# Order and engines at the entry of a hybrid attention and MLP block: column 0 of the scale, the squares of x, TensorE's first work

## The reference

```python
c_act = jax.nn.silu(c)
mod = c_act @ w_ada[l] + b_ada[l]
sh_a, sc_a, gt_a, sh_m, sc_m, gt_m = [m[:, None, :] for m in jnp.split(mod, N_MOD, axis=-1)]
h = rms_norm(x, g_pre_attn[l]) * (1.0 + sc_a) + sh_a
proj = h @ w_in[l]
q_a, k_a, v_a, q_b, ckv, k_pe = [proj[..., offs[i]:offs[i + 1]] for i in range(6)]
...
o = jnp.concatenate([rms_norm(o_a, g_out_a[l]), rms_norm(o_b, g_out_b[l])], axis=-1)
o = o @ w_out[l]
x = x + gt_a * rms_norm(o, g_post_attn[l])
h = rms_norm(x, g_pre_mlp[l]) * (1.0 + sc_m) + sh_m
y = jnp.square(jax.nn.relu(h @ w_mlp_in[l])) @ w_mlp_out[l]
x = x + gt_m * rms_norm(y, g_post_mlp[l])
```

## Time and profile before

| | |
|---|---|
| median of 3 runs | 2016.6 us (2016.35 to 2017.35) |
| the profiled execution, its time | 2017.13 us |
| its span in the profile | 2015.2 us |
| PE busy in the span | 1984.6 us (98%) |
| DVE, ACT busy | 1730.3 us, 1005.1 us |
| granted TensorE clock, mean | 0.998 |

### The profile page before, as it was taken

How to read it: one execution, slowest core, us unless ns; L and a number is a source line. 1 busy time by engine, 2 the same in 40 slices (tenths; PEclk the granted TensorE clock), 3 DMA queues, 4 the chain that set the end, 5 groups by cost and what they waited for, 6 DMA issues and landing times.

```text
span 2015.2 us, 30682 instructions
## 1 busy us (share of the span) xinstructions
PE 1984.6 (98%) x11171; PEld 1738.4 (86%) x11171; DVE 1730.3 (86%) x1993; ACT 1005.1 (50%) x1424; POOL 161.3 (8%) x173
## 2 busy tenths in 40 slices
PE   7999999999999999999999999999999999999998
PEld 5887888788888878999999999998888888888886
DVE  7897998788877788999999999988898898898866
ACT  6464223688733374565656565655343343434322
POOL 0000000257400000000000000000300000000000
PEclk9999999999999999999999999999999999999999
DMA  9988768600378746667676766668746546556452
GB/s 357 369 297 293 237 215 233 214 1 21 130 248 261 239 163 188 206 216 230 214 229 213 229 213 229 214 222 331 255 176 250 193 181 250 186 187 252 175 179 84
DMA packets 260180, 432.28 MB, mean 215 GB/s; under 512 B 27648, under 2 KB 155264, under 8 KB 247168
## 3 DMA queue, kind: packets, MB, share of 16 engines
q1 hardware_dynamic: 242576, 361.42, 53.1%
q0 software_dynamic: 15936, 63.97, 8.6%
q10 hardware_dynamic: 1584, 5.77, 0.8%
HBM read 367.15 MB, written 63.96 MB: 214 GB/s over the span
## 4 chain that ended last, share of the span: by engine, by line
PE 91%; DVE 5%; ACT 3%; issue 1%; DMA 0%; POOL 0%; SPq 0%; POOLq 0%; ACTq 0%; DVEq 0%
PE bank L2817 9%; PE bank L2819 9%; PE bank L2818 9%; PE bank L2839 9%; PE bank L2841 9%; PE bank L2840 9%; PE bank L2324 6%; PE bank L2326 6%; PE bank L2325 6%; PE bank L2900 1%; PE bank L2899 1%; PE bank L2898 1%; PE bank L2337 1%; PE bank L2338 1%; PE bank L2339 1%
## 5 line engine op out<-in xcount | busy, mean ns | idle before, releaser
L1367 ACT ACTIVATE hi<-w 128x1024 fp32r<-128x1024 f32 x168 | 178.4, 1062 | 264.8 <-PE bank L2841 197.8
L2839 PE MATMUL bank<-hi,y_use 128*128 128x512 f32 x784 | 306.6, 391 | 0.0
L2840 PE MATMUL bank<-lo,y_use 128*128 128x512 f32 x784 | 305.1, 389 | 0.0
L2841 PE MATMUL bank<-hi,y_use 128*128 128x512 f32 x784 | 305.1, 389 | 0.0
L1286 ACT ACTIVATE hi<-a 128x1024 fp32r<-128x1024 f32 x196 | 206.6, 1054 | 154.5 <-DVE a L2031 141.9
L2028 DVE TENSOR_TENSOR lo<-a,hi 128x1024 fp32r<-128x1024 f32 x196 | 239.1, 1220 | 43.6 <-ACT hi L1286 43.2
L2817 PE MATMUL bank<-h_hi,hi 128*128 128x256 f32 x896 | 253.7, 283 | 0.9 <-DVE c_b L2058 0.9
L2818 PE MATMUL bank<-h_lo,hi 128*128 128x256 f32 x896 | 253.6, 283 | 0.0
L2819 PE MATMUL bank<-h_hi,lo 128*128 128x256 f32 x896 | 253.6, 283 | 0.0
L819 ACT ACTIVATE hi<-raw 128x1024 fp32r<-128x1024 f32 (+2 forms) x120 | 120.5, 1007 | 230.9 <-DMA raw<-in_w_in 66.6
L2143 DVE TENSOR_TENSOR lo<-w,hi 128x1024 fp32r<-128x1024 f32 x168 | 203.9, 1220 | 32.0 <-ACT hi L1367 30.7
(11 more groups left out here) (402 smaller groups left out, 4700.5 us busy)
## 6 DMA issues: line engine op xcount, KB each, us to landing
w<-in_w_mlp_out SPq DMA_DIRECT2D x128, 512.0 KB, 4.8
a<-in_w_mlp_in SPq DMA_DIRECT2D x112, 512.0 KB, 4.5
y_use<-y_dram SPq DMA_DIRECT2D x53, 1024.0 KB, 9.3
raw<-in_w_ada SPq DMA_DIRECT2D x100, 512.0 KB, 4.7
y_dram<-y_out POOLq DMA_DIRECT2D x28, 1792.0 KB, 6.8
w_turned<-in_w_ada_t SPq DMA_DIRECT2D x32, 1024.0 KB, 7.1
raw<-in_w_out SPq DMA_DIRECT2D x32, 512.0 KB, 4.6
raw<-in_w_heads SPq DMA_DIRECT2D x32, 448.0 KB, 6.5
```

The costliest lines, as they stand in the source:

```text
L1367: nc.scalar.activation(hi[w.slot()][:], weight(np, i, h)[:], ACT.Copy).then_inc(hi_ready, 1)
L2839: mm(bank[b + m][:], yh, hi[s][:, q, :], start=j == 0, stop=False)
L2840: mm(bank[b + m][:], yh, lo[s][:, q, :], start=False, stop=False)
L2841: ins = mm(bank[b + m][:], yl, hi[s][:, q, :], start=False, stop=j == PAIRS - 1)
```

## The change

- `column(0)` is no longer done on DVE. PE does it in 16 matmuls (`first_column`, behind `turn_x(1)`), each with 128x128 of `w_turned` 0 as weights and one column of `silu_c`, into column 0 of bank 6; `w_ada_t` is laid out for it on the host side of the input. DVE's `column_out(0)` reads the bank. The last four transposes of tile 3, which write bank 6, wait for that (`cols_ready`); the wait for `spread_copied` moves from tile 3 to `first_column`.
- ACT takes a root of one element of `ones` behind the Exp, so that its table is loaded there. ACT now copies the banks 6 and 7 of the spread, DVE the banks 4 and 5.
- PE runs 24 matmuls of one column on `ones` before the spread and 24 transposes of `ident` behind it (`WARM = 24`), all into bank 0, which nobody reads.
- ACT squares tiles 1, 2 and 3 each ahead of the copies of an earlier tile, and makes the first `hi` ahead of the root of tile 3. DVE squares tile 1 before it scales tile 0. `h_low(0)` moves behind `column_out(1)`.

```diff
@@ -50,6 +50,7 @@
...
 X_BANK = (7, 4, 5, 6)
+WARM = 24
 TURN_BANK = (4, 5, 3, 7)
@@ -825,7 +826,9 @@
...
             nc.scalar.activation(silu_t[:], gains[:, 0:KD], ACT.Exp, scale=-1.0).then_inc(silu_steps, 1)
-            for m in range(2):
+            act.wait_ge(ones_ready, 1)
+            nc.scalar.activation(stat_s[:, 0, 1:2], ones[:, 0:1], ACT.Sqrt)
+            for m in (2, 3):
                 act.wait_ge(spread, m + 1)
@@ -883,15 +886,18 @@
...
-            for t in range(NT):
-                x_square(t)
-                x_root(t)
-                if t:
-                    if t < NT - 1:
-                        x_copies(t - 1)
-                if t == NT - 2:
-                    x_copies(t)
+            x_square(0)
+            x_root(0)
+            x_square(1)
+            x_root(1)
+            x_square(2)
+            x_copies(0)
+            x_root(2)
+            x_square(NT - 1)
+            x_copies(1)
             start_w_hi(0)
+            x_root(NT - 1)
+            x_copies(2)
             x_copies(NT - 1)
@@ -1470,13 +1476,13 @@
...
             own.step(ts(scale_b[:], bias[:, KD:2 * KD], 1.0, None, ALU.add))
-            for m in (2, 3):
+            for m in range(2):
                 dve.wait_ge(spread, m + 1)
...
-                if n == 0:
+                if n == 1:
                     dve.wait_ge(spread_copied, 4)
@@ -1487,7 +1493,7 @@
...
                 if n < KD:
-                    ts(gsc_a[:, k:k + 1], col_sum[:, n:n + 1], scale_b[:, k:k + 1], gains[:, KD + k:KD + k + 1], ALU.add, ALU.mult).then_inc(cols_ready, 1)
+                    ts(gsc_a[:, k:k + 1], bank[6][:, 0:1] if n == 0 else col_sum[:, n:n + 1], scale_b[:, k:k + 1], gains[:, KD + k:KD + k + 1], ALU.add, ALU.mult).then_inc(cols_ready, 1)
                 else:
@@ -1521,19 +1527,23 @@
...
-            for t in range(NT):
-                if t == NT - 1:
-                    column(0)
-                    column_out(0)
-                x_square(t)
-                x_scale(t)
+            x_square(0)
+            x_square(1)
+            x_scale(0)
+            x_scale(1)
+            x_square(2)
+            x_scale(2)
+            column_out(0)
+            x_square(NT - 1)
+            x_scale(NT - 1)
             start_w_lo(0)
-            h_low(0)
             for n in range(1, CHUNKS):
...
                 column_out(n)
+                if n == 1:
+                    h_low(0)
                 start_w_lo(n)
@@ -2340,8 +2350,10 @@
...
+            pe.wait_ge(ones_ready, 1)
+            for _ in range(WARM):
+                mm(bank[0][:, 0:1], ones[:], ones[:, 0:1], start=True, stop=True)
             pe.wait_ge(const_landed, 32)
-            pe.wait_ge(ones_ready, 1)
             pe.wait_ge(silu_steps, 2)
@@ -2349,6 +2361,17 @@
...
+            for _ in range(WARM):
+                nc.tensor.transpose(bank[0][:, 0:P], ident[:], ident[:])
+
+            def first_column():
+
+                pe.wait_ge(spread_copied, 4)
+                pe.wait_ge(w_turned_landed[0], 16)
+                for k in range(KD):
+                    ins = mm(bank[6][:, 0:1], w_turned[0][:, k * P:(k + 1) * P], silu_c[:, k:k + 1], start=k == 0, stop=k == KD - 1)
+                ins.then_inc(col_summed, 1)
+
             def turn_x(t):
@@ -2356,8 +2379,8 @@
...
                         pe.wait_ge(x_normed, NT + (kk > 0))
-                        if kk == 0:
-                            pe.wait_ge(spread_copied, 4)
+                        if kk == NT - 1:
+                            pe.wait_ge(cols_ready, 1)
                     else:
@@ -2437,6 +2460,8 @@
...
                 turn_x(t)
+                if t == 1:
+                    first_column()
             first_heads()
@@ -3120,7 +3145,8 @@
...
     columns = lambda *rows: np.ascontiguousarray(np.concatenate([r.reshape(-1, P) for r in rows]).T)
-    return {"w_ada_t": np.ascontiguousarray(np.concatenate([w_ada[:, SC_A:SC_A + D].T, w_ada[:, SH_A:SH_A + D].T])),
+    first = w_ada[:, SC_A:SC_A + P].reshape(KD, P, P).transpose(1, 0, 2).reshape(P, D)
+    return {"w_ada_t": np.ascontiguousarray(np.concatenate([first, w_ada[:, SC_A + P:SC_A + D].T, w_ada[:, SH_A:SH_A + D].T])),
             "w_heads": np.ascontiguousarray(np.concatenate([head(h) for h in EARLY], axis=1)),
```

## The result

The changed kernel takes **2020.3 us** (median; 2019.2 to 2021.9) beside 2016.6 for the kernel before: ratio 1.0017, 95% interval 1.0009 to 1.0024, so 1.8 to 4.8 us slower. The forecast was 2014.4, with a range of 2013.0 to 2016.8. The sign was wrong.

What follows compares the result with a forecast made beforehand. PE, busy 98% of the span, was taken as the bound. Entry steps were chained to start chunk 4 2.2 us earlier, carried to the end: profiled execution 2017.13 to 2014.9, median 2014.4 us, range 2013.0 to 2016.8.

Steps and rivals of the forecast that it cites:

- The bound and the yardstick: PE, busy 98% of the span, bounds the kernel; chunk 4's start, 47.73 us before, measures the entry's gain.
- the hole called issue: A later PE wait of 1.6 us with nothing named as its cause, put down to issue.
- Column 0 on PE: Between tiles 1 and 2: 16 one-column matmuls priced at 1.95 us at full pace, where PE waits anyway.
- PE kept running: At PE's entry, extra matmuls and transposes raise the clock; the copies to `silu_b` come 1 to 3 us later.
- Transposes and the clock: At PE's entry: transposes raise the pace, against the skill's rule; tile 0 turned in 1.96 us instead of 3.69.
- Table load: On ACT: the 1.28 us load moves behind the Exp, where ACT waits; priced at nothing.
- squares ahead of copies: On ACT: tile 3 squared as it lands, at 17.4; `h_hi` of chunk 0 comes 1.10 us earlier.
- `h_lo` behind column 1: On DVE: column 1, no longer behind `h_lo` 0, starts at 24.28 against 27.31.
- D: Rival: PE's entry work clogs its queue, neither matmuls nor transposes raising the clock; 6.4 us slower, 2023; chance 0.04.
- B: Rival: PE is at the lower pace when tile 0 comes; gain only 0.7 us, 2015.9; chance 0.15.

Runs made afterwards that it cites:

- e1: The changed kernel without its first loop, the 24 one-column matmuls on `ones`: 2014.4 us, ratio 0.9987.
- f2: e1 without the 24 transposes of `ident` as well, so without both loops: 2016.6 us, ratio 0.9999.
- e2: The changed kernel with only its edits on ACT and DVE; column 0 stays on DVE, no new matmuls on PE: 2015.3 us, ratio 0.9992.
- g1: f1 with 128 equal columns instead of one in column 0's matmuls: 2012.9 us, ratio 0.9979.
- e4: The changed kernel with 128 columns of `ones` instead of one in the first loop: 2016.5 us (one run).
- f1: e1 with tile 3's root right behind tile 1's copies on ACT, and tile 3's square and first high part ahead of `column_out(0)` on DVE: 2015.3 us.
- f3: The kernel before with column 0 alone moved to PE, old order, no loops: 2020.5 us, ratio 1.0020.
- f4: The changed kernel with 128 equal columns instead of one in column 0's matmuls: 2020.3 us (one run).
- g2: f3 with 128 equal columns instead of one in column 0's matmuls: 2018.5 us, ratio 1.0007.
- g3: e1 with 128 equal columns instead of one in column 0's matmuls: 2014.8 us, ratio 0.9988.
- h1: g1 with 40 instead of 24 transposes of `ident` in the second loop: 2013.8 us, ratio 0.9982.
- e3: The kernel before plus only the 24 one-column matmuls on `ones` ahead of the spread: 2023.4 us, ratio 1.0033.

## Why the prediction was wrong

*The bound and the yardstick.* Right in the main: the start of chunk 4 ordered the kernels nearly as their medians did, from 44.35 (2012.9) to 55.52 (2023.4). The sentence that no wait behind it hangs on a transfer was wrong; the hole called issue did, and it swallowed 1.3 of the 4.1 us.

*Column 0 on PE.* The price of 1.95 us was **half of the true one**. The row `bank<-ones,mod_acc` in the earlier trace rows says x16, and I took it for 16 matmuls of the program; its source line runs over eight. Its 16 records are 8 matmuls of two passes. So the 16 of column 0 cost 3.7 us, as measured in every kernel at the full pace. With e1's late tiles taken off, the sum comes behind the 19.7 up to which it was free.

*PE kept running.* This is the step that turned the sign. "24 x 0.12 to 24 x 0.24" should have been 48 passes, and "half of them by the one pace or the other" should have been none at the full one: 10.4 us instead of some 5. It is the step that failed: the loop was priced per matmul of the program, and at a pace that it never reached. I had called this the price that I knew least, and bounded it by the nearest row, but by a row misread. The spread, in whose way the loop stands, was late by 7.6 us instead of 1 to 3, tile 0 came at 18.69 (forecast 12.9), the column was summed at 25.9 (18.4), and root, `h_hi` and chunk 4 were each 6.2 to 6.3 us later than forecast. Of these 6.3 the loop makes 5.3: without it (e1) chunk 4 came at 46.53, 1.2 earlier than before, where 2.2 had been forecast. The dearer column and tiles that landed 0.7 later lie between.

*Transposes and the clock.* Here the trace was the better guide than the page that I had weighed against it. In the changed kernel the pace doubled during the transposes of `ident`, in e1 too, where PE had done nothing but transposes before, and in f2 tile 0 ran at half pace without them. Part 4 of "TensorE: Matmul & The Clock Gate" in the Trainium skill, by which transposes don't bring the full clock, doesn't hold for these.

*Table load, squares ahead of copies, `h_lo` behind column 1.* Right as mechanisms, but the sum gave the squares 1.1 of the 2.2 us, and in e1 and e2 they brought 0.1 at `h_hi` of chunk 0: the root of tile 3 waited for DVE (22.40 and 22.44, forecast 21.42), which squares tile 3 behind column 0. Only in g1, with two more moves, did they pay: `h_hi` came at 23.05, 2.3 us earlier than before. There ACT runs from tile 3's square on as it was laid out, less the first high part, and from the root of tile 3 to `h_hi` of chunk 0 the changed kernel took 2.95 us, where the forecast had 2.81; from `h_hi` 1 to column 2 it took 1.98 (34.06 to 36.04), just as forecast.

*The rivals.* It went as D, PE's entry work in front of the spread and of column 0, which had been given 0.04. Its point of decision, column 0 summed later than 21.9, was right: 25.9. Its time, 2023, was not: it had the transposes at half pace too, and the one-column matmuls at half their price. What made it rare in my eyes was that I tied it to transposes that don't raise the pace; the one-column matmuls sufficed, at two passes each. B had the right doubt (single columns may not raise the pace) with half the price.

## What to carry to other kernels

Before a row prices an instruction, compare its count with the source: a 32-bit matmul that isn't a transpose stood as two records here, and a price read per record is half of it. Work that only keeps an engine running must end before its first real work can start, and it has to be of a kind that the trace shows to raise the pace; the second loop, in idle time, was worth 1.2 us, and the first, ahead of the spread, cost 5.3 in the changed kernel and 7.8 in the one before. Where a step moves to another engine, follow all that stood behind it in both orders: the same column on PE cost 2.6 us at chunk 4 in the old order, and in g1's it ended while ACT had other work.

## What the runs showed of the hardware

- 48 passes of one column, without a gap, left PE at the lower pace for 10.40 us (three executions); with 128 columns it doubled within 8.26 us (one execution). At the same pace a pass takes the same time with 1 or 128 columns: column 0's 32 passes took 3.63 to 3.68 us and 3.74 us.
- During or just behind 3.7 us of single-column passes the granted clock fell from 1.00 to 0.50 in four of six profiled executions (changed kernel, e4, f1, f3; not e1, f2); in e4 it fell 1.4 us behind them, during transposes. During or just behind the same passes with 128 columns it fell in none of five (f4, g1, g2, g3, h1). These are single executions, so the difference can be chance, the medians of e1 and g3, which differ in nothing else, are alike, and why it fell in some only stays open.
- Around idle time the clock fell too, and not always. It fell within the 3.03 us ahead of tile 3 in e3, and 0.8, 1.0 and 1.8 us behind the end of 3.07 us (g2), 2.95 us (g3) and 2.61 us (e2). Behind 3.03 us in the kernel before and 2.62 us in e1 it did not fall.
- At the start of each program the granted clock reads 1.00 while the pace is half; the column shows falls, not the level at the start.
